# A hybrid mixer and MoE kernel: order of the first loads, both blocks transposed ahead of chunk one, overlay tensors at multiples of 128 bytes

## What is computed

```python
def reference(x, norm1_w, w_in, ...):
    for layer in range(2):
        h = rmsnorm(x, norm1_w[layer])
        x = x + hybrid_mixer(h, w_in[layer], ...)     # proj = h @ w_in: 1024 x 3336 columns
        h = rmsnorm(x, norm2_w[layer])
        x = x + (swiglu(h, ...) if layer % 2 == 0 else moe_swiglu(h, ...))
    return rmsnorm(x, final_norm_w)
```

## Time and profile before

| | us |
|---|---|
| time, median of 3 runs (lowest to highest) | 1530.79 (1528.57 to 1532.62) |
| the profiled execution | 1530.88 |
| its span, first to last instruction | 1528.8 |
| PE busy | 1497.1 |
| PEld (weight loads of PE, beside PE) busy | 1243.2 |
| DVE busy | 1175.9 |
| ACT busy | 981.9 |
| POOL busy | 49.0 |

### The profile page before, as it was taken

The page is one execution under the profiler, slowest core; times in us unless marked ns, Lnnn a source line. Parts: engine busy times, 40 slices in busy tenths (PEclk is TensorE's granted clock), DMA queues, the critical chain, the costliest instruction groups (busy, mean ns, idle before and its releaser), DMA issues.

```text
span 1528.8 us, 19222 instructions
## 1 busy us (share of the span) xinstructions
PE 1497.1 (98%) x7309; PEld 1243.2 (81%) x7312; DVE 1175.9 (77%) x844; ACT 981.9 (64%) x757; POOL 49.0 (3%) x53
## 2 busy tenths in 40 slices
PE   7999999999999999999999999999999999999997
PEld 5987788888888878888878888887888888888886
DVE  4777445444687588898878889878889888888886
ACT  4565433334556677777777776776777777777774
POOL 2000000000000000001000000200000200000010
PEclk9999999999999899999999999999999999999999
DMA  9624555554542489999999999999999999999992
GB/s 304 227 99 138 179 192 192 189 186 139 174 165 84 146 287 386 371 357 362 372 334 335 376 370 353 369 342 326 371 373 355 368 373 330 352 368 375 347 375 110
DMA packets 190647, 437.71 MB, mean 286 GB/s; under 512 B 9376, under 2 KB 13536, under 8 KB 190448
## 3 DMA queue, kind: packets, MB, share of 16 engines
q1 hardware_dynamic: 189024, 432.89, 79.3%
q0 software_dynamic: 1120, 2.20, 0.6%
q10 hardware_dynamic: 432, 1.57, 0.3%
HBM read 435.59 MB, written 1.05 MB: 286 GB/s over the span
## 4 chain that ended last, share of the span: by engine, by line
PE 94%; DVE 3%; DMA 1%; ACT 1%; issue 1%; SPq 0%; ACTq 0%; DVEq 0%
PE ps L1295 29%; PE ps L1296 29%; PE ps L1297 29%; PE ps L1587 2%; PE ps L1544 1%; DMA raw<-in_w_in_dram 1%; DVE w_lo L813 1%; PE ps L1562 1%; PE ps L1563 0%; PE ps L1358 0%; PE ps L1357 0%; PE ps L1356 0%; ACT w_hi L465 0%; PE ps L1789 0%; PE ps L1350 0%
## 5 line engine op out<-in xcount | busy, mean ns | idle before, releaser
L1142 DVE TENSOR_TENSOR w_lo<-raw,w_hi 128x2048 fp32r<-128x2048 f32 x333 | 754.6, 2289 | 125.0 <-ACT w_hi L640 122.9
L640 ACT ACTIVATE w_hi<-raw 128x2048 fp32r<-128x2048 f32 x332 | 630.0, 1919 | 173.0 <-PE ps L1297 173.0
L1295 PE MATMUL ps<-w_hi,aT_hi 128*128 128x512 f32 (+1 forms) x1296 | 512.8, 396 | 15.3 <-DVE w_lo L813 7.1
L1297 PE MATMUL ps<-w_hi,aT_lo 128*128 128x512 f32 (+1 forms) x1296 | 504.6, 389 | 0.0
L1296 PE MATMUL ps<-w_lo,aT_hi 128*128 128x512 f32 (+1 forms) x1296 | 504.5, 389 | 0.0
L1295 PEld LDWEIGHTS ps<-w_hi,aT_hi 128*128 128x128 f32 x1296 | 244.3, 189 | 70.4 <-issue 12.7
L1297 PEld LDWEIGHTS ps<-w_hi,aT_lo 128*128 128x128 f32 x1296 | 244.2, 188 | 52.6
L1296 PEld LDWEIGHTS ps<-w_lo,aT_hi 128*128 128x128 f32 x1296 | 244.4, 189 | 48.6
L813 DVE TENSOR_TENSOR w_lo<-raw,w_hi 128x2048 fp32r<-128x2048 f32 (+2 forms) x81 | 176.9, 2186 | 108.1 <-ACT w_hi L465 107.8
L465 ACT ACTIVATE w_hi<-raw 128x2048 fp32r<-128x2048 f32 (+2 forms) x81 | 148.1, 1830 | 112.1 <-PE ps L1297 104.3
L1295 PE MATMUL ps<-w_hi,s2T_hi 128*128 128x512 f32 x544 | 213.5, 392 | 0.0
(11 more groups left out here) (274 smaller groups left out, 920.1 us busy)
## 6 DMA issues: line engine op xcount, KB each, us to landing
raw<-in_moe_w_gate_dram SPq DMA_DIRECT2D x112, 1024.0 KB, 7.0
raw<-in_moe_w_up_dram SPq DMA_DIRECT2D x112, 1024.0 KB, 7.6
raw<-in_moe_w_down_dram SPq DMA_DIRECT2D x112, 1024.0 KB, 7.0
raw<-in_w_in_dram SPq DMA_DIRECT2D x20, 1024.0 KB, 5.7
raw<-in_ffn_w_gate_dram SPq DMA_DIRECT2D x14, 1024.0 KB, 5.1
raw<-in_ffn_w_up_dram SPq DMA_DIRECT2D x14, 1024.0 KB, 5.1
raw<-in_ffn_w_down_dram SPq DMA_DIRECT2D x14, 1024.0 KB, 4.9
raw<-in_w_out_dram SPq DMA_DIRECT2D x8, 1024.0 KB, 5.1
```

The lines of the kernel that those rows point to most:

```text
L640: nc.scalar.activation(moe_hi(pos), raw[:, slot, :], ACT.Copy).then_inc(hi_ready, 1)
L1142: V.tensor_tensor(moe_lo(pos), raw[:, pos % 6, :], moe_hi(pos).bitcast(F32), ALU.subtract)\
L1295: mm(out, lhs_hi, rhs_hi, start=start, stop=False, skip_group_check=True)
L1297: return mm(out, lhs_lo, rhs_hi, start=False, stop=stop, skip_group_check=True)
```

## The change

It changes five things. (1) Loads at the start: SP loads the identity alone (cst[0:C_IOTA]), x block 0 and x block 1, then the weights, without a wait; the rest of cst follows the sixth half (behind chunk 2), and PE waits for it before the first use of the masks. ACT issues the norm weight and the two dt column loads of layer 0. GpSimd waits for the second weight half, then issues the parameters of layer 0, `heads8` first; those of layer 1 and the router weight are issued behind the norm2 load in layer 0. The parameter semaphores are now one for each layer and kind. (2) In layer 0 both blocks are normalised ahead of the splits of chunk 0, and PE transposes both ahead of the first product; the splits of the two halves stand around the copies of block 0; 6 warming matmuls instead of 14. (3) In both layers the transpose of the parameter rows moves behind chunk 1, and the evacuation of xbc follows ACT's copy of it. (4) In both layers the first half of chunk 2 is split ahead of the dt chain. (5) A tensor of 8 floats per partition is placed in front of the overlay region.

```diff
+        align128 = sb("align128", [P, 8])
...
-                        if name == "bvdt":
+                        if name == "bvdt" and l > 0:
                             sp.dma_start(view[:, :, wide:n], dts[half]).then_inc(dt_in[half], 16)
                         g += 1
-                        if g == 3:
-                            sp.dma_start(cst[:, C_COS:], const_d[:, C_COS:]).then_inc(tables_in, 16)
+                        if g == 6:
+                            sp.dma_start(cst[:, C_IOTA:], const_d[:, C_IOTA:]).then_inc(tables_in, 16)
...
-            sp.dma_start(cst[:, 0:C_COS], const_d[:, 0:C_COS]).then_inc(const_in, 16)
-            sp.wait_ge(x_in[0], 16)
+            sp.dma_start(cst[:, 0:C_IOTA], const_d[:, 0:C_IOTA]).then_inc(ident_in, 16)
+            for b in range(NB):
+                sp.dma_start(x[:, b, :], x_d[0, b * P:(b + 1) * P, :]).then_inc(x_in[b], 16)
             mixer_weights(0)
...
-            for l in range(LAYERS):
+            def params(l):
+
                 rows = prm_rows[:, l, :]
...
                 for i, src in enumerate((dt_bias_d, a_log_d, d_skip_d)):
...
+                    pool.dma_start(heads8[:, l, i, :], src[l].partition_broadcast(P)).then_inc(heads_in[l], 16)
...
+            pool.wait_ge(landed[1], 16)
+            params(0)
...
                 pool.dma_start(normw, norm2_d[l].partition_broadcast(P)).then_inc(normw_in, 16)
                 if l + 1 < LAYERS:
+                    params(l + 1)
+                    pool.dma_start(rw[:], router_d[0].rearrange("(k p) e -> p k e", p=P)).then_inc(rw_in, 16)
                     pool.wait_ge(mix_sb, l + 1)
...
-            act.dma_start(x[:, 0, :], x_d[0, 0:P, :]).then_inc(x_in[0], 16)
             act.dma_start(normw, norm1_d[0].partition_broadcast(P)).then_inc(normw0_in, 16)
-            act.dma_start(x[:, 1, :], x_d[0, P:2 * P, :]).then_inc(x_in[1], 16)
+            for half in range(2):
+                act.dma_start(win_view(raw, half, WIN[0][2])[:, :, 256:], dt_cols(0)[half]).then_inc(dt_in[half], 16)
...
                 norm_block(2 * l, 0, ready[0], counts[0])
-                if l > 0:
+                if l == 0:
+                    norm_block(0, 1, ready[1], counts[1])
+                    win_split(l, 0, (0,))
+                    hT(0, 0)
+                    hT(0, 1)
                     win_split(l, 0, (1,))
...
-                act.wait_ge(prm_psum, l + 1)
-                nc.scalar.activation(prm[:], ps[:, 4, 0:PRM_ALL], ACT.Copy).then_inc(prm_ready, 1)
-
+                win_split(l, 2, (0,))
+
+                act.wait_ge(heads_in[l], 48)
                 nc.scalar.activation(sm(3, 8), heads8[:, l, 1, :], ACT.Exp)
...
-                win_split(l, 2)
-                chunk_done(1)
+                win_split(l, 2, (1,))
+                act.wait_ge(prm_psum, l + 1)
+                nc.scalar.activation(prm[:], ps[:, 4, 0:PRM_ALL], ACT.Copy).then_inc(prm_ready, 1)
                 act.wait_ge(pad_set, l + 1)
...
                 if l == 0:
-                    hT(2 * l, 0)
-                    hT(2 * l, 1)
-                    win_split(l, 0)
+                    norm_block(0, 1)
+                    win_split(l, 0, (0,))
+                    hT(0, 0)
+                    hT(0, 1)
+                    win_split(l, 0, (1,))
...
                     transposed_block(0, 0)
-                    keep_warm(0, 14)
+                    transposed_block(0, 1)
+                    keep_warm(0, 6)
...
-                transposed_block(2 * l, 1)
+                if l > 0:
+                    transposed_block(2 * l, 1)
...
-                pe.wait_ge(prm_in, 16 * 8 * LAYERS)
+                win_chunk(l, 1)
+                pe.wait_ge(prm_in[l], 16 * 5)
                 nc.tensor.transpose(ps[:, 4, 0:PRM_ALL], prm_rows[:, l, :], cst[0:PRM_ALL, C_ID:C_ID + PRM_ALL])\
                     .then_inc(prm_psum, 1)
-                win_chunk(l, 1)
                 win_chunk(l, 2)
                 win_chunk(l, 3)
 
                 pe.wait_ge(prm_ready, l + 1)
                 pe.wait_ge(a_ready, l + 1)
+                pe.wait_ge(tables_in, 16)
```

More of the change, by code:

```diff
@@ L223, in hybrid_kernel @@
         dt_in = [sem(f"dt_in{half}") for half in range(2)]
+        heads_in = [sem(f"heads_in{l}") for l in range(LAYERS)]
+        prm_in = [sem(f"prm_in{l}") for l in range(LAYERS)]
         (xT_psum, xtok_ready, xdt_ready, rot_psum, qk_ready) = map(
@@ L247, in win_view, with dt_cols @@
             return buf[:, slot, 0:4 * n].rearrange("p (k n) -> p k n", k=4)
+        def dt_cols(l):
+            return w_in_d[l, :, DT0:DT0 + SH].rearrange("(h k p) n -> h p k n", h=2, k=4)
         def at(pos):
@@ L288, in mixer_weights @@
                 g = MIX_BASE[l]
-                dts = w_in_d[l, :, DT0:DT0 + SH].rearrange("(h k p) n -> h p k n", h=2, k=4)
+                dts = dt_cols(l)
                 for name, c0, n in WIN:
@@ L383, in _ @@
             pool.memset(xbc[:, :, 0:TAPS - 1], 0.0).then_inc(pad_set, 1)
[L384 removed]
+            def params(l):
                 rows = prm_rows[:, l, :]
[L386 to L393 removed]
+                for i, src in enumerate((dt_bias_d, a_log_d, d_skip_d)):
+                    pool.dma_start(heads8[:, l, i, :], src[l].partition_broadcast(P)).then_inc(heads_in[l], 16)
+                pool.dma_start(rows[0:PRM_B], conv_w_d[l].rearrange("k (m c) -> (k m) c", c=P)).then_inc(prm_in[l], 16)
+                pool.dma_start(rows[PRM_B:PRM_N], conv_b_d[l].rearrange("(m c) -> m c", c=P)).then_inc(prm_in[l], 16)
+                pool.dma_start(rows[PRM_N:PRM_N + 2], ret_norm_d[l].rearrange("(m c) -> m c", c=P)).then_inc(prm_in[l], 16)
+                pool.dma_start(rows[PRM_N + 2:PRM], ssd_norm_d[l].rearrange("(m c) -> m c", c=P)).then_inc(prm_in[l], 16)
+                pool.dma_start(rows[PRM:PRM_ALL], norm2_d[l].rearrange("(m c) -> m c", c=P)).then_inc(prm_in[l], 16)
+            pool.wait_ge(landed[1], 16)
+            params(0)
             for l in range(LAYERS):
@@ L491, in mixer @@
                 norm_block(2 * l, 0, ready[0], counts[0])
-                if l > 0:
-                    win_split(l, 0, (1,))
-                hT(2 * l, 0)
-                hT(2 * l, 1)
-                if l == 0:
-                    win_split(l, 0)
-                norm_block(2 * l, 1, ready[1], counts[1])
+                if l == 0:
[3 more added lines that the diff above has]
+                    hT(0, 1)
+                    win_split(l, 0, (1,))
+                else:
+                    win_split(l, 0, (1,))
+                    hT(2 * l, 0)
+                    hT(2 * l, 1)
+                    norm_block(2 * l, 1, ready[1], counts[1])
                 hT(2 * l, 2)
@@ L868, in mixer @@
                     win_split(l, 0, (1,))
-                norm_block(2 * l, 1)
+                    norm_block(2 * l, 1)
                 hT(2 * l, 2)
@@ L872, in mixer @@
                 win_split(l, 1)
-                dve.wait_ge(prm_in, 16 * 8 * LAYERS)
+                win_split(l, 2, (0,))
+                dve.wait_ge(heads_in[l], 48)
                 dve.wait_ge(win_out, 7 * l + 1)
@@ L1854, in _ @@
             keep_warm(0, 20)
-            pe.wait_ge(const_in, 16)
+            pe.wait_ge(ident_in, 16)
             mixer(0)
```

14 lines of the change are left out of this document (2 added, 12 removed).

## The result

Over five runs of each, one beside the other, the changed kernel takes 1516.60 us in the median (1514.14 to 1518.21) where the kernel before takes 1530.62 (1526.08 to 1532.62). The ratio is 0.9913, with a 95% interval of 0.9897 to 0.9928: 14.0 us faster. The forecast was 8.5 us faster, 1522.4, with a range from 1518.5. The direction holds; the size lies outside the range.

What follows compares the result with a forecast made beforehand. PE was taken as the bound, busy 1497.1 of 1528.8 us, with the end following its xbc start. An 8.9 us earlier start less 0.4 for the parameter transpose gave -8.5, from 1530.88 to 1522.4 us; range 1518.5 to 1526.5.

Steps and rivals of the forecast that it cites:

- 1. Loads: Start: weights issued without waiting for x; x0 lands at 5.7, x1 about 7.0, w0 8.8, w1 10.6 us.
- 2. Compute: Work ahead of chunk one: compute alone lets PE start xbc at 18.6, 11.2 us earlier.
- 3. xbc0: First xbc half: GpSimd's parameter loads cost it 3.0 us, landing about 16.6; PE starts at 20.9, gain 8.9.
- B: Rival, start: broadcasts hardly disturb loads outside an empty pipe; PE starts xbc at 18.6, total 1520.1 us; chance 0.20.
- 4. What stays fed: Behind the xbc start: xbc1, tables, rqk0 and head parameters all land in time, no cost.
- 5. The parameter transpose: Both layers, behind chunk one: the transpose is no longer hidden, costing 0.4 us in all (bounds 0.2 and 1.0).
- 6. Layer 1 parameters: Near 90 us: late layer 1 parameter and router loads disturb weight loads briefly; cost zero, above 1.
- 7. Placement: 32 bytes of padding move the fourth split buffer, silu, h and sel; effect zero.
- C: Rival, start: slowest engine lags 4.7 and the clock falls; xbc starts at 22.6, total 1525.8 us; chance 0.11.
- D: Rival, start: weights slow in themselves, not through GpSimd; xbc starts at 24.9, total 1526.4 us; chance 0.08.
- E: Rival, expert stage: new addresses make PE read the fourth buffer worse; 14 ns each give 1536.4 us; chance 0.03.
- F: Rival, later stages: they run at the DMA's pace, so the lead is given back; 1530.5 us; chance 0.03.

Runs made afterwards that it cites:

- e8: Changed kernel with x block 0 issued ahead of the identity on SP; 1516.08 us, ratio 0.9914.
- e16: Changed kernel with the fourth split buffer 128 bytes on and SP's wait for x block 0 back ahead of the weights; 1511.68 us, ratio 0.9870.
- e3: Changed kernel with all sixteen parameter loads and the router load issued by GpSimd from the start; 1523.05 us, ratio 0.9961.
- e2: Changed kernel without the 8 floats (32 bytes) of padding; 1519.17 us, ratio 0.9942.
- e15: Changed kernel with the fourth split buffer 128 bytes on, the same kernel as e9 run again; 1510.68 us, ratio 0.9869.
- e1: Kernel before with only the 8 floats of padding added; 1527.46 us, ratio 0.9995.
- e10: Kernel before with only the fourth split buffer moved 416 bytes further on; 1520.35 us, ratio 0.9937.
- e12: Changed kernel with GpSimd issuing layer 0's eight parameter loads from the start, layer 1's and the router load still late; 1518.91 us, ratio 0.9932.
- e9: Changed kernel with the fourth split buffer 128 bytes further on; 1510.80 us, ratio 0.9872.

## Why the prediction was wrong

*What bounds the kernel.* Half right. PE is saturated from the start of xbc, and that start moved the end one for one. But "31.7 us is all that an edit of order or timing can win as long as the matrix work stays the same" left the padding out of the edits that can shorten matrix work: 9.9 us came out of busy time, 3.0 of them in the expert stage.

*1. Loads.* x0 was forecast at 5.7 and came at 6.71, x1 at 7.0 and came by 8.20, w0 at 8.8 and came at 10.05, w1 at 10.6 and was there at 11.82, when GpSimd's wait for it ended. All are late by 1.0 to 1.25, and the marks of 9.5 and 11.5 for the splits were missed (10.05, 11.99): the byte count alone says nothing of x0's later issue on SP (1.17 instead of 0.73), nor of the identity's 128 pieces of 512 bytes ahead of it, and e8 without both hits 5.66. Harmless, since it shrinks to 0.76 by the start of xbc.

*2. Compute.* Right: 18.6 forecast for a compute-bound start, 19.36 measured, and PE had no idle time right ahead of xbc.

*3. xbc0.* The step of the start that failed: "I take 3.0". xbc0 landed at 14.25, not 16.6. It followed w1 (11.82) by 2.4, so even the undisturbed 2.8 was enough, and the term is 0. Two things kept it from xbc0. The first piece of the parameter loads moved at 15.9, 4.1 us after the first issue and 1.7 after xbc0 had landed. I had put the burst into xbc0 as if it began with the issue; the trace of before has 4.3 us between the two (1.34 and 5.6), and by my own times (issue at 10.6 or later, xbc0 at 13.4) the burst would have begun behind xbc0. That alone takes the stall off xbc0, also in e16, where it came and held up xbc1. And in after it hardly came: q0 had 16.8% in 15 to 17.5, so the mark set in the prediction (q0 holds much of the DMA between 12 and 17) was missed. Why the same loads hold 16.8% in after and 61.9% in e16 is open; that weight loads were queued doesn't explain it, since they were queued in e3, in e16 and in after. The gain at the start was 10.5 instead of 8.9, as B had it.

*4. What stays fed.* Right: behind 19.3 us PE has no wait over 0.5 up to 130.

*5. The parameter transpose.* About right. The transpose and ACT's copy stand on the path to rqk0's split, which ended at 36.58:

```profile
30.97 0.25 PE L1409 MATMUL ps<-cst,prm_rows 44*128 44x44 f32 x1
```

```profile
34.29 2.29 DVE L831 TENSOR_TENSOR w_lo<-raw,w_hi 128x2048 fp32r<-128x2048 f32 x1 [0.41 <-ACT w_hi L478]
```

From the first xbc matmul to the router takes 488.1 us in the executions of the new order with one fall of 3.4 us there (e2, e8, e15, e16; 488.2 in e3) and 487.5 in those of the old order with one (before, e1, e10): 0.6, against 0.4 (0.2 to 1.0) forecast. The falls lie at different places, at 74 and at 451 us, so the 0.6 is an estimate. After's own 486.50 has no fall in it, and that is the 0.96 gained in this stretch: executions of the new order with and without one differ by 1.6 (488.1 and 486.5). Whether the order has a part in it is open: all three executions of the old order had the fall at 451 to 453, and of the fifteen with the new loads none had it there and five had one at 74 to 80.

*6. Layer 1 parameters.* Right, nothing seen: SP waited 755.3 us for the splits of the expert stage, against 758.9 in the earlier trace rows.

*7. Placement.* The second step that failed, and the larger one: "nothing to gain but 24 ns on an engine that waits". I looked at the engine that writes the moved buffer, DVE, and not at the one that reads it a thousand times and bounds the kernel. The spread was in the trace of before: matmuls 234.3 ns apart on one buffer of four. Its price was 2.8 us, and 6.5 more lay beside it, unused by the change.

**The rivals.** B had the right start of xbc; its 1520.1 lacks 3.5 us, of which 2.8 are the placement. Its reason, that the broadcasts only disturb in an empty pipe, isn't borne out: e3 and e16 have the stall with weight loads waiting. C did not occur: no stall ahead of xbc0, and no fall before 511 us in after; falls at 11 to 12 did occur in other kernels, where they cost about 1.5 (21.01 against 19.49). D is refuted: w0 did take 7.9 from its issue (2.11 to 10.05), but in the queue behind x, since issued 4.6 later it takes 3.9 (e16); and w1 was there at 11.82, not at 14.8. E had the right place and the wrong sign: I looked for a clash that the old address avoided, and it was the old address at which the matmuls took longer. F did not occur.

**The two rules.** For the loads of GpSimd the Trainium skill, "DMA: Bandwidth & Descriptors", section "Anatomy of one DMA — SWDGE (gpsimd) path", has no burst that stalls the other queues. I had let the measurement decide against it. In after the result is what follows from it, no stall ahead of PE; in e3, e12 and e16 the stall is there. Its 2.0 us and the bytes are also far below the 4 us that passed here between the first issue and the first piece. On the clock, PE stood idle for 3.20 us in e12 and the granted clock went to 0.50 meanwhile. That agrees with the Trainium skill, "TensorE: Matmul & The Clock Gate", section "Part 1: The HAM clock gate", by which idleness brings the throttle back. But e9 and e15 show one program with and without the fall, with pauses of 2.58 and 2.26, so what a short pause costs has to be read from more than one execution.

**The range.** It ended 1.9 us above the result. With the measured terms (10.5 for the start, 0.6 for the transpose, 2.8 for the placement) the sum is -12.7, 1518.2. The 1.6 that are left are of the size of one fall (488.1 against 486.5); that they are one isn't shown. The range had carried the stall's both ends but no end at all for the placement, whose only mention was a rival for the worse.

## What to carry to other kernels

When a change moves addresses, price it where the bounding engine reads them: group that engine's instructions by buffer, and if one buffer's are some per cent longer than its neighbours', that is a gain waiting (here 9.5 us for one gap of 416 bytes), and a gap of 128 bytes is a cheap experiment. A disturbing load can't hold up what has landed before its first piece moves, here 4 us after the issue, so place the burst in time before pricing it. Its price varied too much here to be carried over from one stretch: a like number of packets held 16.8% to 79.1% of the engines' time. Split a span at marks before explaining a difference, and run the same kernel twice, since 2.5 us of this profile's gain were the clock of one execution.

## What the runs showed of the hardware that I had not expected

- Matmuls that stream a 512-column fp32r tile start every 226.7 ns or every 232.9 to 234.3 ns, depending on where the tile lies. 128 and 384 bytes further on are fast, 256 is as slow as 0, and 32 bytes below that is slower still. The cause in the chip is open.
- 91 packets of GpSimd's queue held 16.8% of 16 DMA engines' time in after (0.80 MB passed in 2.5 us), 93 held 79.1% in e3 (0.28 MB) and 66 held 61.9% in e16 (0.36 MB), each time with weight loads issued and waiting. From the first issue to the first piece 4.0 to 4.4 us passed, in before, after, e3 and e16. What makes the difference is open.
- A load of 0.52 MB lands 1.05 us later behind 128 pieces of 512 bytes than in front of them (6.71 against 5.66), of which 0.43 are its later issue.
- The stretch at half clock behind the router lasts 3.4 or 10.2 us in different executions of one kernel, and makes that stage 12.03 or 14.51 us long; at the start one kernel had a fall behind a pause of 2.58 us in one execution (e9) and none behind 2.26 in another (e15), and started xbc 1.5 later. The two together are of the size of the 4 us by which single runs of a kernel differ.
